# A two-block transformer kernel on one core: the end of the first mixer's attention in another order, turned heads copied ahead of scores, and the first merge's weights spread over partitions by DMA

## The reference

```python
def dilated_mixer(h, w_in, w_out):
    proj = (h @ w_in).reshape(B, S, N_GROUPS, 3, N_HEADS, HEAD_DIM)
    for g, (window, dil) in enumerate(((128, 1), (512, 4), (2048, 16))):
        q, k, v = partial_rotary(proj[:, :, g, 0], pos), partial_rotary(proj[:, :, g, 1], pos), proj[:, :, g, 2]
        o, lse = dilated_band_attention(q, k, v, dil, window // dil)
        outs.append(o); lses.append(lse)
    wts = jax.nn.softmax(jnp.stack(lses, axis=0), axis=0)
    o = jnp.einsum('gbsh,gbshd->bshd', wts, jnp.stack(outs, axis=0))
    return o.reshape(B, S, ATTN_WIDTH) @ w_out
```

## Time and profile before

| what | value |
|---|---|
| median of three runs | 2300.19 us (2296.62 to 2302.95) |
| time of the profiled execution | 2301.07 us |
| its span in the profile | 2299.3 us |
| PE busy | 2227.8 us, 97% |
| DVE busy | 1203.8 us, 52% |
| ACT busy | 816.6 us, 36% |
| POOL busy | 492.5 us, 21% |

### The profile page before, as it was taken

How to read it: one execution, slowest core, us unless ns; L and a number is a source line. 1 busy time by engine, 2 the same in 40 slices (tenths; PEclk the granted TensorE clock), 3 DMA queues, 4 the chain that set the end, 5 groups by cost and what they waited for, 6 DMA issues and landing times.

```text
span 2299.3 us, 26729 instructions
## 1 busy us (share of the span) xinstructions
PE 2227.8 (97%) x10598; PEld 1789.7 (78%) x10598; DVE 1203.8 (52%) x1995; ACT 816.6 (36%) x1360; POOL 492.5 (21%) x335
## 2 busy tenths in 40 slices
PE   8999999998999999999999999999998979999999
PEld 7788886887788888876667888888776857877877
DVE  4656556465654443355457444433788675443443
ACT  4434332434232222233433332322478323323322
POOL 2533234150511011123234110112111141100100
PEclk9999999999899999999999999999999999999999
DMA  4222221222233333332212333333332322222322
GB/s 154 83 65 83 74 83 56 65 77 62 67 98 94 99 98 95 101 102 74 92 56 83 93 100 95 98 101 93 92 94 81 100 69 83 87 78 75 96 71 85
DMA packets 85931, 198.27 MB, mean 86 GB/s; under 512 B 7328, under 2 KB 46496, under 8 KB 85808
## 3 DMA queue, kind: packets, MB, share of 16 engines
q1 hardware_dynamic: 83184, 189.62, 27.1%
q10 hardware_dynamic: 2624, 6.93, 0.9%
HBM read 194.40 MB, written 2.13 MB: 85 GB/s over the span
## 4 chain that ended last, share of the span: by engine, by line
PE 89%; DVE 5%; issue 2%; ACT 2%; POOL 1%; DMA 1%; SPq 0%; DVEq 0%; ACTq 0%; POOLq 0%
PE PS L550 52%; PE PS L596 6%; PE PS L598 5%; PE PS L597 5%; PE PS L621 2%; PE PS L623 2%; PE PS L622 2%; PE PS L1073 2%; PE PS L668 1%; PE PS L678 1%; PE PS L692 1%; PE PS L926 1%; PE PS L916 1%; PE PS L937 1%; PE PS L837 1%
## 5 line engine op out<-in xcount | busy, mean ns | idle before, releaser
L1711 DVE TENSOR_TENSOR WL<-WR,WH 128x1024 fp32r<-128x1024 f32 x353 | 468.2, 1332 | 732.8 <-ACT WH L1121 732.3
L1121 ACT ACTIVATE WH<-WR 128x1024 fp32r<-128x1024 f32 x353 | 371.1, 1056 | 692.0 <-DMA WR<-in_ws 680.9
L550 PE MATMUL PS<-XH,WH 128*128 128x512 f32 x1024 | 404.1, 395 | 18.9 <-ACT XH L1130 12.1
L550 PE MATMUL PS<-XL,WH 128*128 128x512 f32 x1024 | 400.5, 391 | 0.0
L550 PE MATMUL PS<-XH,WL 128*128 128x512 f32 x1024 | 400.5, 391 | 0.0
L550 PEld LDWEIGHTS PS<-XH,WH 128*128 128x128 f32 x1024 | 193.6, 189 | 63.4 <-issue 13.9
L550 PEld LDWEIGHTS PS<-XL,WH 128*128 128x128 f32 x1024 | 193.6, 189 | 41.4 <-issue 1.4
L550 PEld LDWEIGHTS PS<-XH,WL 128*128 128x128 f32 x1024 | 193.5, 189 | 40.5
L596 PE MATMUL PS<-XH,WH 128*128 128x512 f32 x544 | 224.8, 413 | 0.0
L598 PE MATMUL PS<-XH,WL 128*128 128x512 f32 x544 | 214.9, 395 | 0.0
L597 PE MATMUL PS<-XL,WH 128*128 128x512 f32 x544 | 214.3, 394 | 0.0
(11 more groups left out here) (327 smaller groups left out, 3715.9 us busy)
## 6 DMA issues: line engine op xcount, KB each, us to landing
WR<-in_ws SPq DMA_DIRECT2D x281, 512.0 KB, 3.6
WR<-in_ws SPq DMA_DIRECT2D x144, 256.0 KB, 3.2
B_CB<-gates ACTq DMA_DIRECT2D x8, 512.0 KB, 4.5
XTOK<-in_x SPq DMA_DIRECT2D x4, 512.0 KB, 5.9
out<-OUT SPq DMA_DIRECT2D x8, 256.0 KB, 2.0
R_D<-in_decay ACTq DMA_DIRECT2D x4, 256.0 KB, 2.6
GAIN<-in_post ACTq DMA_DIRECT2D x1, 512.0 KB, 4.8
CST<-in_cst SPq DMA_DIRECT2D x1, 256.0 KB, 6.5
```

Of the source, the lines that this page charges most:

```text
L550: mm = pe.matmul(PS[:, bank + o, :], l, r, start=first and kk == 0 and i == 0, stop=last and kk == 1 and i == 2)
L1121: nc.scalar.activation(WH[:, s, :], WR[:, s, :], ACT.Copy).then_inc(hi_ready, 1)
L1711: tt(WL[:, s, :], WR[:, s, :], WH[:, s, :].bitcast(F32), ALU.subtract).then_inc(lo_ready, 1)
```

## The change

It has four parts. (1) The weights of half 0: the turned weight rows are copied by DVE to `A_WROW`, written to DRAM by three ACT-issued DMAs, and for each of the twelve merges two ACT-issued DMAs read a row 64 times into a tile `A_WB` (`fetch`); DVE multiplies `A_O` by `A_WB`, and PE has no part in those merges. (2) The merge of half 1 stays on PE, with a selection matrix `A_SEL` of all 128 rows, built on ACT in phase 6, and the transposed weights have 128 rows. (3) The end of the first mixer is placed anew: the third scores of body 5 come in its 23rd place, phase 6 has a place every 6 matmuls for the first four AO units and 24 in all, and the outputs of body 5 are copied to `A_O` by ACT. (4) In the forgetting mixer DVE copies the turned head ahead of the scores, and ACT copies a complete pair (`values`) first.

```diff
         SPREAD = sb("SPREAD", [P, 4, P], at=squares_at)
-        A_SR = sb("A_SR", [P, T], F32R, at=squares_at + 4 * T)
...
         A_Y = a("A_Y", [P, 4, T])
+        A_SEL = sb("A_SEL", [P, 3, T], F32R, at=a.at)
         A_COS = a("A_COS", [P, T])
...
         A_SIN = a("A_SIN", [P, T])
+        A_SH = a("A_SH", [P, 2, T])
         A_P = a("A_P", [P, 2, 2, T])
         A_PT = a("A_PT", [P, 2, T])
-        A_SH = a("A_SH", [P, 2, T])
         A_MX = a("A_MX", [P, 2, 2, TB])
...
         A_M = a("A_M", [P, TB, 8])
-        A_WG = a("A_WG", [P, TB, 96])
+        A_WG = a("A_WG", [P, TB, P])
         A_MS = sb("A_MS", [P, 8, 64], at=a.at)
+        A_WROW = sb("A_WROW", [P, T], at=a.at)
+        A_WB = [sb("A_WB0", [P, T], at=squares_at + 4 * T), sb("A_WB1", [P, T], at=a.at + 4 * T),
+                sb("A_WB2", [P, T], at=a.at)]
         A_WH = a("A_WH", [P, T], F32R)
         A_WL = a("A_WL", [P, T], F32R)
-        A_W = A_WG[:, :, :].rearrange("p b (g s) -> p g b s", s=32)[:, :, :, 0:8]
+        A_W = A_WG[:, :, :].rearrange("p b (g s) -> p g b s", s=32)[:, 0:3, :, 0:8]
         E32 = sb("E32", [P, 32], at=a.at)
...
         gates = nc.dram_tensor("gates", (NH, T), F32, kind="Internal").ap()
 
         a = Arena()
...
 
-        def merged(half, tiles):
-            return [[("merge", half, t, j)] for t in tiles for j in range(3)]
-        late = scored(5)
         place(1, scored(0), 0, 20)
         place(2, scored(1), 0, 20)
         place(3, scored(2), 0, 17)
         place(3, [[("weights", 0)], [("turn", 0)]], 19, 22)
-        place(4, merged(0, range(4)), 0, 9)
+        first = [("merge", 0, t, j) for t in range(4) for j in range(3)]
+        place(4, [[("fetch", k) for k in range(3)]], 0, 0)
+        place(4, [[first[k]] + ([("fetch", k + 2)] if 1 <= k < 10 else []) for k in range(12)], 2, 15)
         place(4, scored(3), 4, 21)
         place(5, scored(4), 0, 14)
-        place(5, late[:3], 18, 21)
-        place(6, late[3:], 0, 5)
-        place(6, [[("weights", 1)], [("turn", 1)]], 4, 5)
-        place(6, merged(1, (0, 1)) + [[("low", 0)]], 6, 7)
-        place(6, [[("low", 1)]] + merged(1, (2,)), 8, 8)
-        place(6, merged(1, (3,)) + [[("low", 2)]], 9, 9)
-        place(6, [[("low", 3)]], 10, 10)
+        def last(kind, *rest):
+            return (kind, 5) + rest
+
+        def blended(*parts):
+            return [("merge", 1, t, j) for t, j in parts]
+        place(5, [[last("scores", 0)], [last("scores", 1), last("turned", 0, 0)], [last("turned", 0, 1)]], 18, 21)
+        place(5, [[last("scores", 2)]], 22, 22)
+        place(6, [[last("values", 0), last("turned", 1, 0)], [last("turned", 1, 1), last("scores", 3)],
+                  [last("values", 1), last("turned", 2, 0)], [last("turned", 2, 1), ("weights", 1)],
+                  [last("values", 2), last("turned", 3, 0)], [last("turned", 3, 1)],
+                  [last("values", 3), ("turn", 1)], blended((0, 0), (0, 1)), blended((0, 2), (1, 0)),
+                  blended((1, 1), (1, 2)), blended((2, 0)) + [("low", 0)], blended((2, 1), (2, 2)),
+                  blended((3, 0)) + [("low", 1)], blended((3, 1), (3, 2)), [("low", 2)], [], [("low", 3)]], 1, 17)
         for spot in sorted(SPOT):
             entries, SPOT[spot] = SPOT[spot], []
             for entry in entries:
...
             FRONT.append(n)
-            if entry[0] in ("scores", "weights", "turn", "merge"):
...
         place_b(forget_ticks(24, B_ITEMS + 3), 66, 86)
+
+        def turned_first(entry):
+
+            return {"norm": 0, "turned": 1, "scores": 2, "values": 3}.get(entry[0], 4)
+
+        def values_first(entry):
+
+            return 0 if entry[0] == "values" else 1
...
                     for b in range(TB):
-                        mm = pe.transpose(PS[0:96, bank, b * P:(b + 1) * P], A_WG[:, b, :], ident)
+                        mm = pe.transpose(PS[:, bank, b * P:(b + 1) * P], A_WG[:, b, :], ident)
                     mm.then_inc(front_done, 1)
-                elif kind == "merge":
+                elif kind == "merge" and ENTRIES[e][1]:
                     _, half, t, j = ENTRIES[e]
                     g = A_BODIES[3 * half + j][1]
                     pe.wait_ge(sel_ready, 3)
                     pe.wait_ge(front_used, FRONT[ENTRIES.index(("turn", half))] + 1)
-                    rows, cols = slice(32 * g, 32 * g + 8), slice(t * P, (t + 1) * P)
-                    pe.matmul(PS[:, bank, :], A_SR[rows, cols], A_WH[rows, :], start=True, stop=False)
-                    pe.matmul(PS[:, bank, :], A_SR[rows, cols], A_WL[rows, :], start=False, stop=True)\
+                    heads = A_SEL[:, g, t * P:(t + 1) * P]
+                    pe.matmul(PS[:, bank, :], heads, A_WH[:, :], start=True, stop=False)
+                    pe.matmul(PS[:, bank, :], heads, A_WL[:, :], start=False, stop=True)\
                         .then_inc(front_done, 1)
...
                     pe.wait_ge(r_part, 2 * q - 2)
-                half_unit = pair_unit(U["AO"] + q, 0, XH, XL, 2 * (q % 2), True, True, x_ready(1))
-                for i in range(2):
+                half_unit = pair_unit(U["AO"] + q, 0, XH, XL, 2 * (q % 2), True, True, x_ready(1), every=1)
+                for i in range(4):
                     next(half_unit)
-                    for e in SPOT.get((6, 2 * q + i), ()):
+                    for e in SPOT.get((6, 4 * q + i), ()):
                         attend(e)
...
                     nc.scalar.activation(A_PT[:, 1, 0:w], PS[:, T_BANK, 0:w], ACT.Copy).then_inc(pt_copied, 1)
+                elif ENTRIES[e][0] == "values" and ENTRIES[e][1] == 5:
+                    _, m, i = ENTRIES[e]
+                    pair, segs, n = item(m, i)
+                    act.wait_ge(pv_done, n + 1)
+                    if pair == 0:
+                        act.wait_ge(y_sum, 8)
+                    nc.scalar.activation(by_class(A_O[:, m % 4, pair, :], 2), classes_of(PS[:, O_BANK, :], 2), ACT.Copy)\
+                        .then_inc(o_copied, 1)
...
+                    act.wait_ge(front_used, FRONT[e] + 1)
+                    for g in range(3):
+                        act.dma_start(weight_rows_out[8 * g:8 * g + 8, :], A_WROW[32 * g:32 * g + 8, :])\
+                            .then_inc(rows_out, 16)
+                elif ENTRIES[e][0] == "fetch":
+                    k = ENTRIES[e][1]
+                    t, j = divmod(k, 3)
+                    row = 8 * A_BODIES[j][1] + 2 * t
+                    if k == 0:
+                        act.wait_ge(rows_out, 48)
+                    if k >= 3:
+                        act.wait_ge(weighted, k - 2)
+                    for h in range(2):
+                        act.dma_start(A_WB[k % 3][HD * h:HD * h + HD, :],
+                                      weight_rows_out[row + h, :].partition_broadcast(HD)).then_inc(row_in[k % 3], 16)
                 elif ENTRIES[e][0] == "turn":
                     act.wait_ge(front_done, FRONT[e] + 1)
-                    nc.scalar.activation(A_WH[0:96, :], PS[0:96, BANK[e], :], ACT.Copy).then_inc(st_hi, 1)
+                    nc.scalar.activation(A_WH[:, :], PS[:, BANK[e], :], ACT.Copy).then_inc(st_hi, 1)
                 elif ENTRIES[e][0] == "low":
                     t = ENTRIES[e][1]
                     act.wait_ge(y_sum, 8 + 2 * t + 2)
...
-                            rows = slice(32 * g, 32 * g + 8)
-                            nc.scalar.activation(A_SR[rows, :].rearrange("p (h j) -> p h j", h=8),
-                                                 CST[rows, IDENT + 32 * g:IDENT + 32 * g + 8].unsqueeze(2)
-                                                 .to_broadcast([8, 8, HD]), ACT.Copy).then_inc(sel_ready, 1)
                     for e in SPOT.get((m, i), ()):
...
             ao = U["AO"]
-            for i in range(16):
-                split(ao + i // 2 + 4)
+            for i in range(24):
+                split(ao + (i // 4 if i < 16 else i // 2 - 4) + 4)
+                if i == 5:
+                    act.wait_ge(qk_ready, 48)
+                    for g in range(3):
+                        nc.scalar.activation(A_SEL[:, g, :].rearrange("p (h j) -> p h j", h=8),
+                                             CST[:, IDENT + 32 * g:IDENT + 32 * g + 8].unsqueeze(2)
+                                             .to_broadcast([P, 8, HD]), ACT.Copy).then_inc(sel_ready, 1)
...
                 split(bf + 9 + g // 4 + 4)
-                for entry in B_SPOT.get(g, ()):
+                for entry in sorted(B_SPOT.get(g, ()), key=values_first):
...
                 body = 3 * half + j
-                pool.wait_ge(front_used, FRONT[e] + 1)
+                if half:
+                    pool.wait_ge(front_used, FRONT[e] + 1)
+                else:
+                    pool.wait_ge(weighted, 3 * t + j + 1)
...
                     pair, segs, n = item(m, i)
-                    if closes(m, i):
+                    if closes(m, i) and m < 5:
...
                     weigh(half)
```

(40 more changed lines are left out.)

## The result

The changed kernel takes 2273.35 us (median of 4 runs, 2272.20 to 2274.65) where the kernel before takes 2299.93 (4 runs): a ratio of 0.9885 with a 95% interval of 0.9868 to 0.9902, 26.6 us less. The forecast was 2268, with a range of 2257 to 2288. The profiled execution took 2272.71 us, its span is 2270.9.

The account below looks back on a forecast made before the run. PE, busy 97% of the span, was taken as the bound, so only its work, waits and clock count. Terms -13 (body 4), -8 (end of body 5 and phase 6) and -11 (forgetting mixer) sum to -32: 2268 us, range 2257 to 2288.

Parts of the forecast that it names:

- Rival B: End of first mixer gains nothing, as half clock follows the `A_V` and `A_MS` waits: sum -26 to 0, 2276; chance .18.
- term 1: Body 4: half 0's merge matmuls leave PE, with their wait and the half clock behind it: -13 us.
- term 3: Forgetting mixer: PE's 11.6 us of waits for `B_PT` go, .6 us kept for new ones: -11 us.
- The price of transfers: Body 4: fetched weight tiles, issued two places or more ahead of use, were taken to cost nothing.
- DVE does as many multiplications as before: Body 4: DVE's multiplication count stays the same, with an SBUF tile in place of PSUM; no cost in the sum.
- rival D's first half: DVE multiplications of body 4 collide with POOL, +6 to +7 us; the whole rival: 2275 to 2283, chance .12.
- Term 2: End of body 5 and phase 6: -17.3 us of waits and half clock, +8.4 of new waits, taken as -8.
- The walk: End of body 5 and phase 6, new order with old durations: waits 3.1 (`A_V`), 3.4 (`A_MS`), 1.9 (merges), 8.4 in all.
- about 1 us of half clock: End of body 5 and phase 6: allowance for lower clock behind one of the two new waits, `A_V` or `A_MS`.
- 7 us of half clock: Phase 6 before: lower-clock loss expected to go, counted from at most 8.8 us because part lies under waits.
- 128 rows cost nothing: Half 1's merge: matmul distance of .23 us doesn't depend on rows; lost side-by-side running, 5.5 us, was called already counted.
- Rival D's second half: Forgetting mixer: scores' maximum, behind the copy, delays exponentials 1 to 1.5 us at up to 8 places, +8; whole rival's chance .12.

Follow-up runs that it names:

- late_fetch: The changed kernel with the nine later weight-tile transfers issued one place, not two, ahead of their multiplication: 2273.46 us, ratio 0.9881.
- weighting_last: The changed kernel with DVE multiplying `A_O` behind the masks and the turned-head copy at each place of body 4: 2272.28 us, ratio 0.9880.
- filled_wait: The changed kernel with 12 useless matmuls on PE ahead of its wait for `A_MS`: 2269.98 us, ratio 0.9872.
- the two edits: The changed kernel, separately with ACT copying `A_V` ahead of the third item's exponentials (2267.65 us) and DVE forming `A_MS` ahead of `WL` (2269.05 us).
- old_places: The changed kernel without part 3 (body 5 and phase 6 placed as before, outputs copied by DVE): 2273.02 us, ratio 0.9883.
- copy_first_alone: The kernel before with part 4 alone (forgetting mixer: DVE copies the turned head first, ACT the complete pair first): 2287.36 us, ratio 0.9944.
- rows_alone: The kernel before with parts 1 and 2 alone, in the old places, without copy first: 2285.27 us, ratio 0.9933.

## Why the prediction was right, and where it was off

The direction and the range were right, the likeliest value 5 us too low; by stage two terms were too large and one too small. Rival B's sum, -26, came out within a microsecond, but in part by luck: it shared my term 1, 4.3 too large, and my term 3, 1.7 too small.

**Term 1, -13 forecast, -8.7 measured.** PE's merge matmuls and their waits went as counted: PE's busy time fell by 7.9 us at the same mean clock. The half clock behind the old wait went too, and as much came behind a new one. The price of transfers, set at nothing, was right: `late_fetch` shows slack. The step that failed is the sentence that DVE does as many multiplications as before, to which the sum gave no price. DVE's 140 instructions of this body take 62.80 us instead of 57.95: the twelve multiplications 11.3 instead of 8.0, the steps `A_ST` 8.0 instead of 5.8, both standing behind POOL. And the order plays in (`weighting_last`): the multiplications stand ahead of the masks, and PE, which no longer spends time on merges, comes to the transposes earlier. Two waits, 1.9 and 1.2 us, and 8 matmuls at half clock (1.6 us) make 4.7, the missing 4.3. Of rival D's first half (+6 to +7) the mechanism was seen, with three collisions of twelve, and where D didn't look, on `A_ST`.

**Term 2, -8 forecast, -3.1 measured.** The walk was good: 3.1 us forecast for `A_V`, 2.5 measured; 3.4 for `A_MS`, 3.2; 1.9 for the merges, .5 + .3 + 1.1. One wait of .8 for the residual sum (L776) was not foreseen. Idle time in all fell from 10.3 to 8.3, where 8.4 was forecast. Two terms failed. The first is "about 1 us of half clock" behind the two waits: the mean clock of .94 over 82.13 us is 4.9, and it lies behind both. That is rival B's mechanism, and B's -1 to -2 for this term is nearer than my -8; `filled_wait` and the two edits show it. I had also counted 7 us of half clock in the stage before where the clock gives 8.5, so that 3.6 went and not 6. The second is the work itself. I wrote that the 5.5 us of merges that no longer run side by side were in the walk, but the sum, -17.3 + 8.4, has no term for them. Without idle time and lost clock the stage holds 66.4 us before and 68.9 after, +2.5. So -2.0 (idle), -3.6 (clock) and +2.5 (work) make the -3.1.

I also wrote that 128 rows cost nothing. In the old places they cost that work and bring more back in clock, 4.8 to 6.5 us net with 1.7 of chance in it; in the new places the two forms can't be told apart. In the old places, then, part 2 alone gave this stage its gain, and part 3 as it stands added nothing (`old_places`), which no term of mine said.

**Term 3, -11 forecast, -12.7 measured.** The mechanism was right and the new waits small (1.3 us for `B_PT` from ACT, .9 for `B_MX`, which was there before). I counted only waiting time, which fell by 9.9 net of new waits; PE's busy time fell by 2.8 as well. Rival D's second half, scores late behind the copy, did not happen.

**Left open.** The profiles differ by 3.9 us where the change does nothing. In the recurrent layer the profile of before has 24.71 us at clock .93 for work that the changed kernel does in 21.98 at 1.00; `copy_first_alone` too was faster there, by 1.6. Of the 2.7, 1.7 is half clock that the profile of before alone has, among fourteen. The rest is a wait of PE for ACT (`L_R`): 2.4 us before and in `copy_first_alone`, 1.0 to 1.4 in the other twelve kernels, all of which have part 1. It doesn't follow from when the layer begins, since `copy_first_alone` and `rows_alone` come to it within 1.1 us of each other; what in the changed first mixer shortens it stays open.

## What to carry to other kernels

When PE is the bound, take its clock into the price of every new wait: here waits of 2.5 and 3.2 us mostly brought 1.6 to 3.4 us more behind them, so a wait can cost up to twice its length. Work taken off the bounding engine has to be placed in the queue of the engine that takes it, behind whatever the bounding engine waits for, and away from POOL if it reads two SBUF tiles; look in the trace for small DVE steps that end just behind a POOL instruction, too. A moved step is looked at on each engine that it crosses: both new waits of part 3 were one instruction in the wrong order on ACT or DVE, and worth 10 us together.

## What the runs showed of the hardware

- Merges of 8 rows instead of 128, in the same places beside waits of 2 to 3 us, lowered the mean granted clock of the stretch from .96 to .88 (40 projection matmuls at 1.2 GHz instead of 16, seven of them ahead of the first merge). Not separated is what does it, the rows themselves, or that 8-row merges of different groups run side by side and leave PE idle for longer (10.4 us against 8.7).
- The same wait of 1.9 us in body 4 was followed by 7 or 8 slow matmuls in six kernels and by none in three (`rows_alone`, `old_places`, `filled_wait`), with nothing changed near it. A stage's profile carries 1.6 us of chance from this alone.
- A transfer that reads a row 64 times into 64 partitions (128 KB) lands in 3.4 us (2.7 to 4.8 over 24 of them), where the weight units of 256 KB land in 3.2 and those of 512 KB in 3.6.
- A DVE step on two elements per partition, with one SBUF input, took .17 us alone and up to 1.0 when it started inside a POOL multiplication or addition in body 4, ending .02 to .03 us behind it (ten of 16).
